# A squared-ReLU MLP in split fp32: two of eight weight pieces of a block by Strassen's seven products

## The reference

```python
x = x + merged @ w_out
h2 = _rms(x, norm2_g)
x = x + jnp.square(jax.nn.relu(h2 @ w_up)) @ w_down
```

## Time and profile before

| | us |
|---|---|
| median of 3 runs (1657.33 to 1658.58) | 1658.3 |
| the profiled execution, its time | 1657.57 |
| the profiled execution, its span | 1655.8 |
| TensorE busy in the span | 1645.6 |
| VectorE busy | 911.1 |
| ScalarE busy | 749.9 |

### The profile page before, as it was taken

How to read it: one execution, slowest core, us unless ns; L and a number is a source line. 1 busy time by engine, 2 the same in 40 slices (tenths; PEclk the granted TensorE clock), 3 DMA queues, 4 the chain that set the end, 5 groups by cost and what they waited for, 6 DMA issues and landing times.

```text
span 1655.8 us, 19903 instructions
## 1 busy us (share of the span) xinstructions
PE 1645.6 (99%) x7472; PEld 1362.9 (82%) x7472; DVE 911.1 (55%) x1001; ACT 749.9 (45%) x875; POOL 4.8 (0%) x13
## 2 busy tenths in 40 slices
PE   8999999999999999999999999999999999999998
PEld 7888888888888888888888888888888888888887
DVE  5856666555565444456665555545555555555553
ACT  6744445444444444443444544434443444334432
POOL 0000000000000000000000000000000000000000
PEclk9999999999999999999999999999999999999999
DMA  9756555566566666665655665666666665665564
GB/s 354 257 166 190 158 174 165 153 178 170 170 183 189 191 192 194 194 192 181 198 184 187 184 187 179 195 195 188 184 191 192 191 188 181 196 193 184 184 189 152
DMA packets 159856, 313.49 MB, mean 189 GB/s; under 512 B 9520, under 2 KB 9648, under 8 KB 159280
## 3 DMA queue, kind: packets, MB, share of 16 engines
q1 hardware_dynamic: 159792, 312.62, 61.8%
HBM read 310.49 MB, written 2.10 MB: 189 GB/s over the span
## 4 chain that ended last, share of the span: by engine, by line
PE 99%; DVE 0%; ACT 0%; DMA 0%; issue 0%; DVEq 0%; SPq 0%; ACTq 0%
PE bank L1028 95%; PE bank L1045 2%; PE bank L1057 1%; PE bank L1151 0%; PE bank L1082 0%; PE bank L1112 0%; DVE wlo L674 0%; PE bank L1171 0%; DMA wide<-in_mem_t 0%; ACT whi L443 0%; PE bank L1077 0%; PE bank L1173 0%; DVE wide L746 0%; ACT L497 0%; PE bank L1083 0%
## 5 line engine op out<-in xcount | busy, mean ns | idle before, releaser
L674 DVE TENSOR_TENSOR wlo<-raw,whi 128x1024 fp32r<-128x1024 f32 x576 | 704.4, 1225 | 674.6 <-ACT whi L443 671.4
L443 ACT ACTIVATE whi<-raw 128x1024 fp32r<-128x1024 f32 x576 | 610.4, 1060 | 780.1 <-PE bank L1028 773.0
L1028 PE MATMUL bank<-whi,lhs_a 128*128 128x512 f32 x1920 | 597.6, 392 | 0.0
L1028 PE MATMUL bank<-whi,lhs_b 128*128 128x512 f32 x1536 | 477.3, 392 | 2.7 <-DVE wlo L674 2.7
L1028 PEld LDWEIGHTS bank<-whi,lhs_a 128*128 128x128 f32 x1920 | 357.1, 188 | 71.8
L1028 PE MATMUL bank<-wlo,lhs_a 128*128 128x512 f32 x960 | 374.2, 390 | 0.0
L1028 PEld LDWEIGHTS bank<-whi,lhs_b 128*128 128x128 f32 x1536 | 287.0, 188 | 61.3 <-issue 3.0
L1028 PE MATMUL bank<-whi,act_parts 128*128 128x512 f32 x1024 | 316.1, 390 | 0.0
L1028 PE MATMUL bank<-wlo,lhs_b 128*128 128x512 f32 x768 | 299.8, 390 | 0.0
L1028 PEld LDWEIGHTS bank<-whi,act_parts 128*128 128x128 f32 x1024 | 191.7, 188 | 39.4
L1028 PEld LDWEIGHTS bank<-wlo,lhs_a 128*128 128x128 f32 x960 | 180.2, 188 | 38.3
(11 more groups left out here) (127 smaller groups left out, 462.7 us busy)
## 6 DMA issues: line engine op xcount, KB each, us to landing
raw<-in_w_in SPq DMA_DIRECT2D x208, 512.0 KB, 3.7
raw<-in_w_up SPq DMA_DIRECT2D x128, 512.0 KB, 3.7
raw<-in_w_down SPq DMA_DIRECT2D x128, 512.0 KB, 3.8
raw<-in_w_mem_kv SPq DMA_DIRECT2D x32, 512.0 KB, 5.8
raw<-in_w_out SPq DMA_DIRECT2D x32, 512.0 KB, 3.8
raw<-in_w_conv_out SPq DMA_DIRECT2D x16, 512.0 KB, 4.4
raw<-in_w_fox_out SPq DMA_DIRECT2D x16, 512.0 KB, 4.6
raw<-in_w_mem_out SPq DMA_DIRECT2D x16, 512.0 KB, 4.0
```

Of the source, the lines that this page charges most:

```text
L443: act.activation(whi[n % RING][:], raw[n % RING][:], ACT.Copy).then_inc(hi_ready, 1)
L674: dve.tensor_tensor(wlo[n % RING][:], raw[n % RING][:], whi[n % RING][:].bitcast(F32), ALU.subtract).then_inc(lo_ready, 1)
L1028: last = pe.matmul(dst, lhs[:, part, k + kk, s], w[:, kk, :], start=(k + kk == 0 and i == 0), stop=(k + kk == tiles - 1 and i == 2))
```

## The change

Of the eight pieces of every MLP block, the third and the fourth (`FAST = 2`, `FASTS = 2`) are computed by Strassen's scheme in Winograd's form. The piece (two row tiles by two halves of 256 columns) is one 2x2 matrix of blocks, the activations (two token tiles by two row tiles) the other. Seven products of 128x128 by 128x256 stand for eight, each again three matmuls with split parts: 21 matmuls of 256 columns for 12 of 512. For this:

- VectorE makes four sums T of the weight blocks of both pieces (`t_sums`), ScalarE their hi parts, VectorE their lo parts, in place of the splits of the first of the four blocks (`split_fast`; the other three are split as before, for both pieces in one instruction).
- Four sums S of the activations are made once per quarter, for the down blocks (`a_copy`, `s_sums`, `s_hi`, `s_lo`), and once for all up blocks.
- The sums of a block take four banks: two as before, in which the ordinary pieces and three of the products add up, and two for four further products (two of them added into one half bank). `combine` makes from these a correction `both` of 128x1024 at the block's last piece, `results` adds it to the first two banks (into `stage`, or for a down block into `x_sb`, for which x has been added to `both` before by `x_to_sums`).
- ScalarE takes relu from `stage` and the square too. The eight transposes of an up block stand together before the next block's fourth piece, in the third and fourth bank of the block they come from. The whole MLP is written as `quarter(q, i)`, called once and then in the loop.
- `act_parts` shares memory with `lhs_a`, and new tiles (t_raw, t_hi, t_lo, S, comb) share it with buffers of the earlier stages.

The core of the diff:

```diff
         @block.scalar
+            def a_copy(bk, u, gain=None):
+                for j in range(PK):
+                    last = act.activation(a_raw[:, u, 2 * j:2 * j + 2, :],
+                                          bank[bk][:, 256 * j:256 * (j + 1)].rearrange("p (t n) -> p t n", t=TOK),
+                                          ACT.Copy, scale=1.0 if gain is None else
+                                          col[:, gain + j:gain + j + 1])
+                last.then_inc(a_copied, 1)
+            def s_hi(i, dst, base=0):
+                act.wait_ge(s_made, base * 4 + 4 * (i + 1))
+                act.activation(dst[:, 0], s_raw[:], ACT.Copy).then_inc(s_hi_ready, 1)
+            def split_fast(n, k, base=0, base16=0, basek=0):
+                act.wait_ge(t_made, basek * 3 + 3 * (k + 1))
+                act.activation(t_hi[:], t_raw[:], ACT.Copy).then_inc(t_hi_ready, 1)
+                for u in range(FASTS):
+                    act.wait_ge(landed[(n + u) % RING], base16 + 16 * ((n + u) // RING + 1))
+                act.wait_ge(piece_used, base + (n + FASTS - RING))
+                r = n % RING
+                act.activation(whi_all[:, r:r + FASTS, HALF_COLS:], raw_all[:, r:r + FASTS, HALF_COLS:],
+                               ACT.Copy).then_inc(hi_ready, FASTS)
+            def quarter(q, i):
+                ...
+                for m in range(2 * NBD * PPB):
+                    k, p = divmod(m, PPB)
+                    if p == FAST:
+                        split_fast(n0 + m, k0 + k, base=by_n, base16=i * (8 * NBD * PPB), basek=by_g)
+                    elif p != FAST + 1:
+                        split(n0 + m, base=by_n, base16=i * (8 * NBD * PPB))
+                    if q == 0:
+                        wo_events(n0 + m)
+                    if p == PPB - 1:
+                        act.wait_ge(piece_used, by_n + (n0 + PPB * k + FAST + FASTS))
+                        act.wait_ge(dve_emptied, by_g + emptied(b0 + k - 1))
+                        act.activation(comb[:, 3, :], bank[ff_set(k) + 2][:, HALF_COLS:],
+                                       ACT.Copy).then_inc(p1_copied, 1)
+                    for k in range(NBD):
+                        e = PPB * k + PPB - 1
+                        if m == e + 5:
+                            ...
+                            act.wait_ge(dve_emptied, by_g + emptied(b0 + k))
+                            for tok in range(TOK):
+                                act.activation(stage[:, tok, :], stage[:, tok, :], ACT.Relu,
+                                               scale=r_2[:, tok:tok + 1]).then_inc(relu_ready, 1)
+                            act.wait_ge(relu_ready, by_g + TOK * (u0 + k + 1))
+                            act.activation(stage[:], stage[:], ACT.Square).then_inc(sq_ready, 1)
+                        for a in range(2):
+                            g, at = g0 + 2 * k + a, 2 * k + a
+                            if m == e + 7:
+                                if FAST <= at < FAST + FASTS:
+                                    act.wait_ge(tr_made, by_g + (g + 1))
+                                    a_copy(ff_set(k) + 2 + a, at - FAST)
+                                plain_hi(g, PK * at, act_parts, bk=ff_set(k) + 2 + a, base=by_g)
+                        if k == 1 and m == e + 10:
+                            s_hi(q + 1, s_down, base=i)
         @block.vector
+            def s_sums(i, base=0):
+                ...
+                dve.wait_ge(a_copied, base * 2 + 2 * (i + 1))
+                dve.tensor_tensor(s1, a21, a22, ALU.add).then_inc(s_made, 1)
+                dve.tensor_tensor(s3, a11, a21, ALU.subtract).then_inc(s_made, 1)
+                dve.wait_ge(s_made, base * 4 + (4 * i + 1))
+                dve.tensor_tensor(s2, s1, a11, ALU.subtract).then_inc(s_made, 1)
+                dve.wait_ge(s_made, base * 4 + (4 * i + 3))
+                dve.tensor_tensor(s4, a12, s2, ALU.subtract).then_inc(s_made, 1)
+            def t_sums(n, k, base16=0, basek=0):
+                for u in range(FASTS):
+                    dve.wait_ge(landed[(n + u) % RING], base16 + 16 * ((n + u) // RING + 1))
+                ...
+                dve.tensor_tensor(t_raw[:, :, 0:2, :], b[:, :, 1:3, :], b12,
+                                  ALU.subtract).then_inc(t_made, 1)
+                dve.wait_ge(t_made, basek * 3 + (3 * k + 1))
+                dve.tensor_tensor(t_raw[:, :, T_2, :], t_raw[:, :, T_1, :], b22, ALU.add).then_inc(t_made, 1)
+                dve.wait_ge(t_made, basek * 3 + (3 * k + 2))
+                dve.tensor_tensor(t_raw[:, :, T_4, :], b21, t_raw[:, :, T_2, :],
+                                  ALU.subtract).then_inc(t_made, 1)
+            def split_fast(n, k, base=0, basek=0):
+                r = n % RING
+                dve.wait_ge(t_hi_ready, basek + (k + 1))
+                dve.tensor_tensor(t_lo[:], t_raw[:], t_hi[:].bitcast(F32), ALU.subtract).then_inc(t_lo_ready, 1)
+                dve.wait_ge(hi_ready, base + (n + FASTS))
+                dve.tensor_tensor(wlo_all[:, r:r + FASTS, HALF_COLS:], raw_all[:, r:r + FASTS, HALF_COLS:],
+                                  whi_all[:, r:r + FASTS, HALF_COLS:].bitcast(F32),
+                                  ALU.subtract).then_inc(lo_ready, FASTS)
+            def combine(k, kk, base=0):
+                ...
+                dve.tensor_tensor(comb[:, 4, :], p6, comb[:, 3, :], ALU.add).then_inc(combined, 1)
+                ...
+                dve.tensor_tensor(comb[:, 1, :], p7, comb[:, 4, :], ALU.add).then_inc(combined, 1)
+                ...
+                dve.tensor_tensor(comb[:, 0:3:2, :], comb[:, 1:5:3, :],
+                                  p5.unsqueeze(1).to_broadcast([P, 2, HALF_COLS]),
+                                  ALU.subtract).then_inc(combined, 1)
+            def x_to_sums(j, kk, base=0):
+                dve.wait_ge(combined, base * 3 + 3 * (kk + 1))
+                dve.tensor_tensor(both, both, x_sb[:, :, COLS * j:COLS * (j + 1)], ALU.add).then_inc(x_in, 1)
+            def results(k, b, base=0):
+                dve.wait_ge(piece_used, base * PPB + (end(b) + 1))
+                at = ff_set(k)
+                dst = stage[:] if k < NBD else x_sb[:, :, COLS * (k - NBD):COLS * (k - NBD + 1)]
+                dve.tensor_tensor(dst, bank_all[:, at:at + TOK, :], both, ALU.add).then_inc(dve_emptied, 1)
+            def quarter(q, i):
+                ...
+                    if p == FAST:
+                        split_fast(n0 + m, k0 + k, base=by_n, basek=by_g)
+                    elif p != FAST + 1:
+                        split(n0 + m, base=by_n)
+                    if p == FAST - 2:
+                        t_sums(n0 + m + 2, k0 + k, base16=i * (8 * NBD * PPB), basek=by_g)
+                    if q == 0:
+                        wo_events(n0 + m)
+                    if p == 2 and (k or q):
+                        ...
+                        results((k - 1) % (2 * NBD), b0 + k - 1, base=by_g)
+                    if p == PPB - 1:
+                        combine(k, k0 + k, base=by_g)
+                        if k >= NBD:
+                            x_to_sums(k - NBD, k0 + k, base=by_g)
+                        else:
+                            dve.wait_ge(combined, by_g * 3 + 3 * (k0 + k + 1))
+                    for k in range(NBD):
+                        e = PPB * k + PPB - 1
+                        for a in range(2):
+                            if m == e + 7:
+                                plain_lo(g0 + 2 * k + a, PK * (2 * k + a), act_parts,
+                                         bk=ff_set(k) + 2 + a, base=by_g)
+                        if k == 1 and m == e + 9:
+                            s_sums(q + 1, base=i)
+                        if k == 1 and m == e + 11:
+                            s_lo(q + 1, s_down, base=i)
         @block.tensor
+            def fast_products(n, u, at, k, lhs, sums, base=0):
+                pe.wait_ge(lo_ready, base + (n + FASTS))
+                ...
+                for dst, a, w, opens, closes in ((bank[at + 2][:, right], a11, b11, True, False),
+                                                 (bank[at + 1][:, right], a12, b21, False, False),
+                                                 (bank[at + 1][:, left], s4, b22, False, False),
+                                                 (bank[at][:, right], a22, t[3], False, False),
+                                                 (bank[at + 3][:, right], s1, t[0], True, False),
+                                                 (bank[at + 2][:, left], s2, t[1], False, True),
+                                                 (bank[at + 3][:, left], s3, t[2], False, True)):
+                    for i, (part, w_part) in enumerate(((1, 0), (0, 0), (0, 1))):
+                        last = pe.matmul(dst, a[part], w[w_part], start=(opens and u == 0 and i == 0),
+                                         stop=(closes and u == FASTS - 1 and i == 2))
```

(69 more changed lines are left out.)

267 lines of the change are left out of this document (151 added, 116 removed).

## The result

The kernel after takes 1667.8 us (median of 4 runs, 1664.3 to 1670.9) against 1658.4 for the kernel before (1657.3 to 1658.7): ratio 1.0059, interval 1.0047 to 1.0072. It is 0.6% slower, where 0.3% faster was forecast. Its own runs spread over 6.6 us, those of the kernel before over 1.4.

The account below looks back on a forecast made before the run. TensorE, busy 99% of the span, was taken as the bound: -13.2 (fast pieces) - 1.9 (transposes) + 1.2 (small waits) + 9.6 (fourth-up-block stall) = -4.3, so 1653.3 us against a median before of 1658.3; range 1643 to 1668.

Parts of the forecast that it names:

- The fast piece at 0.12 a matmul: On TensorE, 21 matmuls of 256 columns at 0.1197 each take 2.51 us a piece against 2.72.
- rival C: On TensorE, weight loads don't overlap with 256 columns, so a fast piece takes 3.95 us: 1735 in all; chance 0.03.
- The stream: TensorE's matmul stream: 64 fast pieces save 13.2 us, putting each up block's eight transposes together saves 1.9.
- The stall of the fourth up block behind s_hi: t_hi queued behind s_hi on ScalarE makes TensorE wait before piece 2 and the transposes: 2.4 a quarter, +9.6 us.
- The second to fourth down blocks: Down blocks: TensorE was to meet no stall at the first fast piece, with a slack of 1.0 us.
- The chain that decides: From piece 7's wlo through the load it releases, T and results to the transposes: TensorE at 18.55 against 18.83.
- It takes 3.7 to land: In that chain, the load of the next block's piece 3 lands 3.7 us after issue, at 6.3 (6.45 in the loop).
- rival B: Piece 3's load decides in every up block; landing 4.6 instead of 3.7 gives +7.1, 1664.7 (1661 to 1675); chance 0.27.
- the slack of 0.3 (0.15 in the loop): Spare time in up blocks between the chain's end and TensorE's start on the transposes before piece 3.
- the twelve groups of the 1.2: Transposes for the first, second and fourth up blocks' results, four quarters: 0.1 us wait each, +1.2 (bounds 0 and 9.0).
- the likeliest case: The main forecast for the whole kernel: 4.3 us faster, between 1649 and 1661; chance 0.48.

Follow-up runs that it names:

- e4: Kernel after with t_sums, t_hi and t_lo made for each of the two fast pieces by itself: 1651.2 us, ratio 0.9959 to the kernel before.
- e8: Kernel after with T made by piece and s_sums, s_hi and s_lo placed behind combine: 1650.6 us, ratio 0.9959 to the kernel before.
- e12: Kernel after with T made by piece, s_sums behind piece 4, s_hi and s_lo at piece 7, loop kept: 1646.4 us, ratio 0.9939.
- e1: Kernel after with s_sums, s_hi and s_lo moved behind the fourth up block's fast pieces: 1663.9 us, ratio 1.0042 to the kernel before.
- e2: Kernel after with every MLP weight load bringing only half its columns (256 KB for 512): 1653.4 us, ratio 0.9975 to the kernel before.
- e6: Kernel after with wlo of the two fast pieces made by two instructions, each freeing its raw slot at once: 1669.2 us, ratio 1.0066.
- e11: Kernel after with only the S sums moved (s_sums behind piece 4, s_hi and s_lo at piece 7): 1657.3 us, ratio 1.0001.
- e13: Kernel after with only the load of each block's fourth piece bringing half its columns: 1656.2 us, ratio 0.9991 to the kernel before.
- e7: Kernel after with s_sums, s_hi and s_lo placed behind combine at the fourth up block's end: 1660.0 us, ratio 1.0013.

## Why the prediction was wrong

**What held.** The fast piece at 0.12 a matmul: 2.52 each, with 42 on end and changing operands, so rival C falls. The rule of the Trainium skill ("TensorE: Matmul & The Clock Gate", "The mechanism") that a weight load overlaps matmuls in flight only when their row groups differ is not borne out here either: 0.12 from start to start is less than the 0.19 of one load. The stream is 13.8 us shorter (forecast 13.2 + 1.9 = 15.1). The stall of the fourth up block behind s_hi: forecast +9.6 (the working gave 2.2 to 2.3 a quarter and 2.4 was taken), measured 10.7, in the two places named. The second to fourth down blocks: no wait but 0.3 here and there. VectorE is busy 78 to 79% of the time in the MLP.

**The step that failed** is in "The chain that decides": "It takes 3.7 to land". I took the landing from the steady spacing of the kernel before, as a constant, and held against rival B that the load in question "leaves alone, 3 us behind its neighbour". It did not stay at 3.7, and it goes with what left shortly before. From the trace's issue and landing events (medians over the up blocks after the first block; the load of piece 3 is the one in question):

```
                        piece 1   piece 2   piece 3   piece 6   piece 7
before: us since the
  load before             2.72      3.21      3.18      2.72      4.06
before: to landing        3.91      3.69      3.69      3.68      3.68
after: since the load
  before                  3.53      1.14      2.67      4.81      0.62
after: to landing         3.84      4.07      4.05      3.83      4.60
```

For the down blocks piece 3's load takes 4.54 (before 3.72), 2.5 us behind one that itself followed another by 2.0. VectorE and ScalarE now make two or three wlo in a row and then none for 4 us, so loads leave in bunches, and one in or behind a bunch lands 0.4 to 0.9 later. All MLP loads after the first block say the same: in the profile after, the 97 that left less than 2.0 behind another have a median of 4.66, the 90 that left 3.5 or more behind one 3.77; in that of before, 16 left less than 2.0 behind another, with a median of 4.63, and the other 232 had 3.7.

From the end of piece 7's wlo to the start of t_sums the profile after has a median of 4.56, 3.85 to 5.16, over all 31 blocks; this is the issue (0.03, in the loop 0.16), the landing, and 0.09 from the landing to t_sums that I had left out. Over the twelve groups of the 1.2 the mean is 4.41, where I had 3.73, in the loop 3.87. What goes beyond this, less the slack of 0.3 (0.15 in the loop), comes block by block to 4.7 us, and in eleven of the twelve groups it meets the measured wait within 0.1. The twelfth is the second block of the first quarter: of its 2.3 only 0.1 is the landing, and the rest comes from piece 7's wlo, which was 2 us late behind the squares and the root of the norm, a piece of work that I had looked at only for its own block. So the twelve groups for which I took 1.2 cost 7.2 (5.8 and 1.4). In the four others the landing ran 1.0 over, which is the 10.7 in place of 9.6. It was rival B's mechanism at a smaller size: the landing is 4.5 of the miss, which makes of 4.3 faster about as fast as before. It is the largest term, but it alone would not have made the kernel slower.

**The second miss** was absent from the prediction: 3.5 us at the start of the third and fourth quarter, where TensorE waits 1.6 to 1.9 at the first piece for "issue" or a wlo long made. The kernel before has a loop over the same three quarters and no such wait. Written out it goes. In the looped kernels e4, e8 and e12 2.3 to 2.4 remain, but in another place: before the first fast piece, for a wlo that is late because VectorE has stood in "issue" for 2.7 to 2.9 at its own edge.

The traces point to the fetching of instructions, which the profile lists as DMA packets. The first three lines below count the packets of queue q8 (16 KB each): in the loop's first turn (1100 to 1290) before, in the same stretch after, and in the two later turns (1290 to 1640) after, where before has none at all. Then come TensorE at the edge of after and VectorE at that of e12:

```profile
q8 instruction: 7, 0.11, 0.2%
...
q8 instruction: 8, 0.13, 0.3%
...
q8 instruction: 18, 0.29, 0.3%
...
1301.24 0.72 PE L1408 MATMUL bank<-whi,lhs_b 128*128 128x512 f32 x2 [1.56 <-issue]
...
1285.94 1.23 DVE L758 TENSOR_TENSOR wlo<-raw,whi 128x1024 fp32r<-128x1024 f32 x1 [2.70 <-issue]
```

So TensorE's part of the loop was fetched once before and then run three times, if q8 is TensorE's queue, and after it is fetched again in each turn. At the twelve edges at which TensorE waits 0.7 or more (after, e1, e2, e6, e11, e13), its first matmul comes 2.57 to 2.68 us after the start of such a packet (1298.56 and 1301.24 here); at the eight edges of e4, e7, e8 and e12 the packet started 2.9 to 3.2 before, and there it waits 0.3 or nothing. The written-out kernels fetch all the way too, and without a jump they don't wait. Where VectorE stands at its edge, as in e12, there are packets of queue q14 as well: 8 in the two later turns, none there before and after. No run varied the length of the loop's code by itself, so this is the trace's reading and not an experiment's.

Together 6.0 (7.2 less the 1.2) + 3.5 + 1.1 (fourth block) + 1.5 (other) + 1.3 (stream) + 0.6 (start) = 14.0; -4.3 and this make +9.7. My chance for slower was 0.26, and that 1667.8 lies within rival B's 1661 to 1675 is in part luck, as 9 of the 14 come from terms that B did not have (the edge, the first quarter's blocks, the stream, the start). The error was to give the likeliest case a slack smaller than the scatter of the row on which it stood, 0.15 against a landing whose rows ran from 3.4 to 9.1, and to price that at 0.1; the other was to look at no edge.

What I can't show is why bunched loads land later. The mean share of the DMA engines is no higher than before (60.3% against 61.8% of the span), but it swings. In 40 slices of 1100 to 1290, in tenths, before and after:

```profile
DMA  6666676675565576574756647466556656655576
...
DMA  3786339723766239760368643974339833695339
```

Slices at 9 tenths would fit loads that share busy engines; no run tests it. A deeper ring, which might take the landing off the chain altogether, wasn't tried.

## What to carry to other kernels

Fewer columns for more helper work pays only if the helpers' chain keeps slack: sum the chain from the event that frees a buffer, through the load that it releases, to the instruction that TensorE waits for, and don't trust a slack that is smaller than the scatter of one of its terms. What is short on a nearly full engine is not its total but the place: with the four sums behind t_sums the fourth up blocks wait 10.7 us, with s_lo ahead of the releasing wlo the next blocks wait 8.7, and in a gap of 2 us, with T by piece, the sums cost nothing. Cutting an operation in two, so that only half of it stands behind the late load, made VectorE busier and the kernel 16.6 us faster.

## What was unexpected in the hardware's behaviour

Loads of 512 KB that leave 0.6 behind another land after 4.6 to 4.7 us in the profile after (medians of piece 7), those 3.5 or more behind one after 3.8; loads of 256 KB (e2) have medians of 2.7 and 2.9. Matmuls of 256 columns run 0.12 apart for 42 on end although each weight load takes 0.19. A loop's edge that cost nothing before cost 1.6 to 1.9 us here, where code was fetched anew in each turn of the loop and not only in the first.
